# A down GEMM that hands over its banks one by one, with half of the next norm's sums inside its last round

## The reference, cut to what matters

```python
def rmsnorm(x, g):
    y = xf * lax.rsqrt(jnp.mean(xf * xf, axis=-1, keepdims=True) + NORM_EPS)
    return (y * g).astype(x.dtype)

def swiglu(h, w1, w3, w2):
    return (jax.nn.silu(h @ w1) * (h @ w3)) @ w2       # D_FF = 2816

x = x + g2 * rmsnorm(ffn(h), norm_g[l, 3])             # the end of layer 0
h = modulate(rmsnorm(x, norm_g[l, 0]), sh1, sc1)       # layer 1 begins
... h @ w_in of the odd mixer, attention, a mixture of 8 experts ...
```

## Time and profile before

| | us |
|---|---|
| runs: median (lowest, highest) of 3 | 2242.49 (2241.3, 2245.68) |
| profiled execution: span | 2240.4 |
| busy PE / DVE / ACT | 2015.4 / 1433.3 / 1210.4 |
| last round of the down GEMM starts | 802.23 |
| banks are copied from | 807.87 |
| square root of n3 starts | 821.73 |

### The profile page before, as it was taken

How to read it: one execution, slowest core, us unless ns; L and a number is a source line. 1 busy time by engine, 2 the same in 40 slices (tenths; PEclk the granted TensorE clock), 3 DMA queues, 4 the chain that set the end, 5 groups by cost and what they waited for, 6 DMA issues and landing times.

```text
span 2240.4 us, 25373 instructions
## 1 busy us (share of the span) xinstructions
PE 2015.4 (90%) x9386; PEld 1603.1 (72%) x9386; DVE 1433.3 (64%) x1355; ACT 1210.4 (54%) x1227; POOL 68.4 (3%) x124
## 2 busy tenths in 40 slices
PE   4699778699999977878979999999999999999996
PEld 3587546488887846853768878788787878878785
DVE  3545473633323336455458888888888888888885
ACT  3644353433322236433537767676777777776773
POOL 0011000000000000113000000000000000000000
PEclk9899889899999988986959999999999999999998
DMA  8455202143332214521028989899998989899891
GB/s 277 149 170 174 72 1 75 38 151 125 122 112 94 94 38 146 190 81 31 22 94 330 365 308 368 307 362 336 348 361 307 367 313 364 323 353 361 314 364 51
DMA packets 266582, 473.49 MB, mean 211 GB/s; under 512 B 19416, under 2 KB 119056, under 8 KB 266512
## 3 DMA queue, kind: packets, MB, share of 16 engines
q1 hardware_dynamic: 262928, 469.33, 59.5%
q0 software_dynamic: 3456, 3.19, 0.6%
q10 hardware_dynamic: 128, 0.03, 0.0%
HBM read 471.27 MB, written 1.05 MB: 211 GB/s over the span
## 4 chain that ended last, share of the span: by engine, by line
PE 79%; DVE 11%; ACT 5%; issue 3%; DMA 1%; ACTq 0%; SPq 0%; DVEq 0%; POOL 0%
PE bank L478 22%; PE bank L479 22%; PE bank L480 22%; PE bank L527 2%; PE bank L646 2%; DVE split_low L462 2%; ACT split_high L457 2%; PE bank L347 2%; DVE overlay L371 2%; PE bank L1657 2%; DVE split_low L1421 2%; ACT overlay L406 1%; PE bank L621 1%; PE bank L1699 1%; PE bank L636 1%
## 5 line engine op out<-in xcount | busy, mean ns | idle before, releaser
L1421 DVE TENSOR_TENSOR split_low<-raw_weights,split_high 128x2048 fp32r<-128x2048 f32 x224 | 511.7, 2287 | 59.8 <-ACT split_high L1115 58.8
L1115 ACT ACTIVATE split_high<-raw_weights 128x2048 fp32r<-128x2048 f32 x224 | 429.3, 1920 | 147.7 <-PE bank L480 147.7
L462 DVE TENSOR_TENSOR split_low<-raw_weights,split_high 128x1024 fp32r<-128x1024 f32 x214 | 256.9, 1224 | 372.2 <-ACT split_high L457 372.1
L478 PE MATMUL bank<-h_high,split_high 128*128 128x512 f32 (+1 forms) x848 | 329.3, 388 | 47.6 <-DVE h_low L392 30.5
L457 ACT ACTIVATE split_high<-raw_weights 128x1024 fp32r<-128x1024 f32 x214 | 219.5, 1051 | 227.9 <-PE bank L480 210.8
L479 PE MATMUL bank<-h_low,split_high 128*128 128x512 f32 (+1 forms) x848 | 322.8, 381 | 0.0
L480 PE MATMUL bank<-h_high,split_low 128*128 128x512 f32 (+1 forms) x848 | 322.7, 381 | 0.0
L1421 DVE TENSOR_TENSOR h_low<-raw_weights,h_high 128x2048 fp32r<-128x2048 f32 x112 | 256.7, 2292 | 78.7 <-ACT h_high L1115 78.6
L478 PE MATMUL bank<-split_high,xe_high 128*128 128x512 f32 x672 | 272.2, 405 | 14.0 <-DVE split_low L1421 14.0
L479 PE MATMUL bank<-split_low,xe_high 128*128 128x512 f32 x672 | 267.6, 398 | 0.0
L480 PE MATMUL bank<-split_high,xe_low 128*128 128x512 f32 x672 | 265.2, 395 | 0.0
(11 more groups left out here) (242 smaller groups left out, 3028.9 us busy)
## 6 DMA issues: line engine op xcount, KB each, us to landing
raw_weights<-in_moe_w SPq DMA_DIRECT2D x336, 1024.0 KB, 6.6
raw_weights<-in_w_mod SPq DMA_DIRECT2D x48, 1024.0 KB, 5.3
raw_weights<-in_ffn_w SPq DMA_DIRECT2D x33, 1024.0 KB, 5.2
raw_weights<-in_ev_w_in SPq DMA_DIRECT2D x10, 1024.0 KB, 5.8
raw_weights<-in_od_w_in SPq DMA_DIRECT2D x8, 1024.0 KB, 5.6
raw_weights<-in_ev_w_out SPq DMA_DIRECT2D x4, 1024.0 KB, 5.5
raw_weights<-in_od_w_out SPq DMA_DIRECT2D x4, 1024.0 KB, 5.3
overlay<-in_rpb SPq DMA_DIRECT2D x32, 64.0 KB, 2.3
```

Source lines behind the costliest of these rows:

```text
L462: dve.tensor_tensor(half_of(s, j, SPL[:, s % NSPLIT, :]), half_of(s, j, raw_of(split_at[s])), half_of(s, j, SPH[:, s % NSPLIT, :]).bitcast ...
L478: pe.matmul(ps, wh, xh, start=first, stop=False)
L1115: act.activation(esplit(u)[0], RAW[:, u % NRAW, :], ACT.Copy).then_inc(S("e_high"), 1)
L1421: dve.tensor_tensor(lo, RAW[:, u % NRAW, :], hi.bitcast(F32), ALU.subtract)\
```

## The change

The last matmul of each bank in the last round raises `gk_used`, so that it counts 21 for the rounds before and then one for each bank, 29 in the end; `unit_used` of the last down unit waits for 29. DVE makes all eight copies, each as soon as its bank is done; ACT's four copies are gone. A square waits for its own copy only. TensorE issues sum t of n3 behind the matmuls of bank t + 4 for t = 0 to 3, and sums 4 to 7 behind the round. Because all eight banks are in use during the round, the sums of n3 go to bank 0, which has been copied by then.

```diff
-            "n3": norm("n3", KT, ys(0), TOK, D, ("ffn_evac", lambda t: KT)),
+            "n3": norm("n3", KT, ys(0), TOK, D, ("ffn_evac", lambda t: t + 1), bank=0),
...
             if s in of["down"]:
-                return S("gk_used"), 2 * of["down"].index(s) + 2
+                d = of["down"].index(s)
+                return S("gk_used"), 2 * d + (9 if d == FT // 2 - 1 else 2)
...
-            act.wait_ge(S("gk_used"), FT)
-            for m in range(4):
-                act.activation(Y[:, m, :], PS[m][:, :], ACT.Copy).then_inc(S("ffn_evac"), 1)
             act_squares(act, N["n3"])
...
-            dve.wait_ge(S("gk_used"), FT)
-            for m in range(4, 8):
+            for m in range(KT):
+                dve.wait_ge(S("gk_used"), FT + m)
                 dve.tensor_copy(Y[:, m, :], PS[m][:, :]).then_inc(S("ffn_evac"), 1)
...
                                      k == 0, k == FT - 1)
-                    last.then_inc(S("gk_used"), 1)
-            pe.wait_ge(S("ffn_evac"), 8)
-            pe_sums(pe, N["n3"])
+                        if k == FT - 1:
+                            last.then_inc(S("gk_used"), 1)
+                            if m >= 4:
+                                pe_sum(pe, N["n3"], m - 4)
+                    if k < FT - 1:
+                        last.then_inc(S("gk_used"), 1)
+            for t in range(4, KT):
+                pe_sum(pe, N["n3"], t)
             pe.wait_ge(*norm_root("n3"))
```

## The result

The changed kernel takes 2228.74 us (median of five runs, 2228.0 to 2234.86), the kernel before 2243.15 us beside it (five runs, 2241.3 to 2245.68): ratio 0.9943, 95% interval 0.9929 to 0.9956. That is 14.4 us less, where 6.8 us were forecast. In the two profiled executions the span fell from 2240.4 to 2226.9 us, by 13.5 us. Groups of 16 to 22 runs of the kernel before, taken later, have medians of 2240.6 to 2241.4 us: the five beside the first result lie some 2 us higher.

What follows compares the result with a forecast made beforehand. TensorE was taken as the bound, with the serial chain of copies, sums and root behind the down GEMM on the path. Saving 3.4 us by order and 3.4 by clock: 2242.5 - 6.8 = 2235.7 us, range 2232.3 to 2240.7.

Steps and rivals of the forecast that it cites:

- Steps (a) to (d): Last down round to n3's square root: signals cost 0, DVE keeps up, PE never waits in the round, root at 814.95.
- Step (e): n3's square root starts at 814.95 instead of 821.73, saving 6.8 us: 3.4 by order, 3.4 by clock.
- order: Part of the n3 saving: the new order beats the old sums at full clock throughout by 3.4 us.
- clock: Part of the n3 saving: without a pause in front of the sums the clock does not fall, 3.4 us.
- Step (f): Behind n3: nothing else is late next; shifts of later clock falls bounded by 3.4 us either way, taken as 0.
- second rival: Gain given back behind n3 as starts shift against half clock: 3.4 us a stretch, two give 2242.5; chance 0.11.
- third rival: Sums in PE's queue stall the last down round: 9.8 us slower, 2252.3; chance 0.06.

Runs made afterwards that it cites:

- fill: Kernel before the change, with six unneeded matmuls on PE in the pause between the last down round and n3's sums: 2232.64 us, ratio 0.9965.
- warm_before: Kernel before the change, with one unneeded matmul in each of the 16 steps of layer 1's attention: 2239.03 us, ratio 0.9991.
- again_after: The changed kernel unaltered, in a later group of four runs: median 2230.57 us, ratio 0.9956 to the kernel before beside it.
- hold3_before: Kernel before the change, with three unneeded DVE operations directly ahead of layer 1's attention, for which PE waits: 2242.95 us.
- hold4_after: The changed kernel with four unneeded DVE operations directly ahead of layer 1's attention, for which PE waits: 2238.13 us.
- before: The kernel before the change, with nothing added: 2243.15 us beside the first result, 2240.63 to 2241.36 us in four later groups.
- hold1_before: Kernel before the change, with one unneeded DVE operation directly ahead of layer 1's attention, for which PE waits: 2241.44 us.
- hold4_before: Kernel before the change, with four unneeded DVE operations directly ahead of layer 1's attention, for which PE waits: 2235.34 us, ratio 0.9970.

## Why the prediction was wrong

- Steps (a) to (d), signals, copies, sums in the round and the tail: right. Forecast from round to root 12.72 us, measured 12.95. The seams that I took at nothing cost a little: bank and sum together take 806.30 - 804.73 = 1.57 us, where I had 0.68 + 0.86 = 1.54, and the tail from the sum behind bank 7 to the root 4.87 us instead of 4.70.
- Step (e), the saving of 6.8 us: 6.55 measured in the profiled pair, 3.7 of it order and 2.9 clock (forecast 3.4 and 3.4). The old sums at full clock, taken as 6.9 us, take 7.6 to 7.7 us in `fill` and `warm_before`, where squares and sums wait for each other. It is not the same in every execution; where the clock does not fall in the pause, as in `warm_before`, only the order half is there.
- Step (f), "whether that and later falls come 6.8 us earlier too, or a little more or less, I bound by what the one stretch of half clock in n3 costs (3.4 us, step e), either way, and take 0": this is the step that failed. In the profiled pair it was worth 6.0 us: -2.37 in the odd mixer, 6.59 in attention, 1.06 and 0.70 behind it. The half clock did not just come earlier: in attention it went from 38 to 18 us. The bound was read from n3, where eight sums follow each other. The stretch that needed pricing was attention, where half clock can go on for 38 us and costs 3.56 us for every two steps. The row for it stood in the earlier trace rows, a mean clock of 0.76 over 200 us at which I priced only one more stretch like that of n3.
- The second rival had the mechanism, and said that a shift is as likely to gain as to lose. It got 0.11 and a price of 3.4 us a stretch; only its losing side had a chance of its own. With 6 us below the forecast the range would have reached down to 2229.7, and 2228.74 would still have missed it. The rest is luck of the first runs: with `again_after` the median is 2230.57 us, inside such a range though outside the stated one, and the gain 10.8 us. That attention moved in favour of the change and not against it is luck too, as far as the prediction goes: it had no way to tell.
- The third rival, stalls in the round: excluded, no PE row in the round has an idle bracket.

What stays open: why attention holds the half clock for so long from some starts and not from others, and whether the pattern of the starts holds beyond these thirteen profiles; two of the aimed shifts (`hold3_before`, `hold4_after`) missed. The extra 1.1 us behind attention come with a mean clock of 0.74 in place of 0.71, the 0.7 us in the experts with 4.1 us at half clock at their start in place of 5.8; neither was tested.

## What to carry to other kernels

A chain of copy, square and sum behind a GEMM costs PE a pause; signal each bank when it is done, and here the pause went, whether the next work is put inside the round or right behind it. Where a stage far behind a change runs for long at a mean clock well below 1, a shift of a few microseconds can move it by as much as the change gains: price that stage from its own rows at both clocks, on both sides, before believing a sum. And compare such kernels stage by stage, since a total of 13.5 us held 6.6 us of the change and 6 us of clock.

## What the runs showed of the hardware

The granted clock stayed at 0.50 through stretches in which PE was nearly always busy. Kernel before, in attention:

```profile
1024.00:1034.00 10.00, 9.58 (x20) 3.92 (x20) 4.38 (x11) 3.04 (x7) 2.90 (x4) 0.50 0.12 25
...
1050.00:1060.00 10.00, 7.63 (x32) 3.87 (x32) 7.17 (x19) 4.61 (x10) 3.87 (x6) 1.00 0.19 39
```

A share of 96% at half clock and 76% at full clock belong to the same loop: the half clock held for 44 us there, from 6 us ahead of attention, and the full clock for the rest of it. So a busy PE is no sign of a PE at its peak; why it was not granted the full clock is not shown. And the same pause of 3.33 us brought the clock down in some executions and not in another. The three profiles in which it cost the full 2.9 us (`before`, `hold1_before`, `hold3_before`) start the round 111.2 to 111.3 us behind the clock's last rise; `hold4_before`, which lost 1.4 us, 111.1 us; `warm_before`, which lost nothing, 112.1 us. The Trainium skill (TensorE: Matmul & The Clock Gate, What's actually happening) has the monitor run free of the kernel's start, which these executions agree with: up to there their code is the same, and these distances are not.
